# A delta-rule layer's triangular inverse: its 16x16 diagonal blocks solved on VectorE through memory, TensorE's doublings from 16 on

## The reference, cut to what matters

```python
a_mat = jnp.where(strict, jnp.einsum("bhncd,bhnmd->bhncm", kb, k) * decay, 0.0)
t_mat = a_mat + jnp.eye(cs, dtype=f32)
rhs = jnp.concatenate([v * beta[..., None], kb * jnp.exp(gc)[..., None]], axis=-1)
sol = lax.linalg.triangular_solve(t_mat, rhs, left_side=True, lower=True, unit_diagonal=True)
...
v_new = u_i - jnp.einsum("bhcd,bhde->bhce", w_i, s)
o_i = jnp.einsum("bhcd,bhde->bhce", q_i, s) + jnp.einsum("bhcm,bhme->bhce", qk_i, v_new)
s = s * d_i[..., None, None] + jnp.einsum("bhcd,bhce->bhde", k_i, v_new)
```

## Time and profile before

| what | value |
| --- | --- |
| median of 3 runs | 3300.11 us (3296.35 to 3301.86) |
| profiled execution: its own time | 3295.26 us |
| its span, first to last instruction | 3293.5 us |
| mean granted TensorE clock | 0.976 |
| TensorE (PE) matmul busy | 3108.8 us, 94% of the span |
| TensorE weight load (PEld) busy | 2038.3 us, 62% |
| VectorE (DVE) busy | 1745.3 us, 53% |
| ScalarE (ACT) busy | 1522.9 us, 46% |
| GpSimd (POOL) busy | 775.7 us, 24% |
| DMA engines, mean share | 24.6% |
| masked copies of the inverse on VectorE (L1319, L1321) | 502.8 us |

### The profile page before, as it was taken

How to read it: one execution, slowest core, us unless ns; L and a number is a source line. 1 busy time by engine, 2 the same in 40 slices (tenths; PEclk the granted TensorE clock), 3 DMA queues, 4 the chain that set the end, 5 groups by cost and what they waited for, 6 DMA issues and landing times. The chain is left out here.

```text
span 3293.5 us, 56323 instructions
## 1 busy us (share of the span) xinstructions
PE 3108.8 (94%) x22057; PEld 2038.3 (62%) x22057; DVE 1745.3 (53%) x3545; ACT 1522.9 (46%) x3283; POOL 775.7 (24%) x588
## 2 busy tenths in 40 slices
PE   5878999999999999999999999796999999999998
PEld 2346777777777764455545565443777777777753
DVE  1136666666666652244442344344667767766632
ACT  3135555555555541145532444333556555555521
POOL 0033433333343220001101011003343434343300
PEclk9689999999999999999999999998999999999999
DMA  9911211221121027012302111202122212121135
GB/s 375 321 56 44 70 51 56 60 60 56 48 73 56 29 70 264 3 53 63 132 18 49 33 46 41 82 11 72 49 62 64 64 52 72 52 75 53 43 118 191
DMA packets 224099, 261.97 MB, mean 80 GB/s; under 512 B 19418, under 2 KB 158948, under 8 KB 223716
## 3 DMA queue, kind: packets, MB, share of 16 engines
q1 hardware_dynamic: 223844, 258.46, 24.6%
HBM read 239.15 MB, written 19.27 MB: 78 GB/s over the span
## 5 line engine op out<-in xcount | busy, mean ns | idle before, releaser
L894 PE MATMUL ps<-hT,W 128*128 128x512 f32 (+1 forms) x2656 | 997.4, 506 | 3.2 <-DVEq L192 2.0
L894 PEld LDWEIGHTS ps<-hT,W 128*128 128x128 f32 x2656 | 470.4, 192 | 200.8 <-issue 171.6
L1319 DVE CAST_PREDICATED arena<-mask,ps 128x384 bf16<-128x384 uint32 x448 | 252.6, 564 | 201.7 <-PE ps L963 166.2
L1144 ACT CAST arena<-ps 128x384 bf16<-128x384 f32 x384 | 167.0, 482 | 339.0 <-PE ps L950 338.0
L2355 PE MATMUL ps<-arena 128*128 128x512 f32 x712 | 309.5, 592 | 2.6 <-SPq L192 2.4
L1321 DVE CAST_PREDICATED arena<-mask,ps 128x384 bf16<-128x384 uint32 x448 | 250.2, 558 | 0.0
L2355 PEld LDWEIGHTS ps<-arena 128*128 128x128 f32 x712 | 133.9, 190 | 166.4 <-issue 161.7
L1990 PE MATMUL ps<-hT,W 128*128 128x512 f32 (+1 forms) x608 | 218.2, 493 | 0.8 <-DMA W<-in_att_w_in 0.5
L1431 POOL TENSOR_TENSOR arena<-arena,cst 128x768 f32<-128x768 f32 x64 | 117.1, 1852 | 386.6 <-DVE arena L1288 384.0
L1300 DVE SCALAR_TENSOR_TENSOR arena<-arena,vec 128x770 f32<-128x770 f32 (+1 forms) x192 | 196.2, 1022 | 6.8
L961 PEld LDWEIGHTS ps<-arena 128*128 128x128 bf16 x2304 | 153.1, 98 | 42.4 <-issue 32.5
(11 more groups left out here) (279 smaller groups left out, 6112.5 us busy)
## 6 DMA issues: line engine op xcount, KB each, us to landing
arena<-in_ada_w SPq DMA_DIRECT2D x24, 2048.0 KB, 19.5
W<-in_gdn_w_in SPq DMA_DIRECT2D x95, 512.0 KB, 4.0
arena<-decay_sums SPq DMA_DIRECT2D x64, 384.0 KB, 4.1
W<-decay_rows SPq DMA_DIRECT2D x64, 384.0 KB, 5.1
arena<-in_gdn_w_out SPq DMA_DIRECT2D x32, 512.0 KB, 10.6
W<-in_gdn_w_out SPq DMA_DIRECT2D x30, 512.0 KB, 3.5
arena<-gated SPq DMA_DIRECT2D x32, 384.0 KB, 8.0
gated<-arena SPq DMA_DIRECT2D x24, 384.0 KB, 2.3
```

The source lines that it names most:

```text
L894: mm = pe.matmul(ps[:, b, 0:t1 - t0], w[:, i, :], env.hT[:, i, t0:t1], start=(i == 0), stop=(i == KD - 1))
L1144: act.copy(half_cols(Xb[d], s, d), ps[:, 2 * d, 0:384].rearrange("p (c b s) -> p c b s", c=NT, s=s)).then_inc(*inxe.up(m, lv, d))
L1319: dve.copy_predicated(half_cols(Mb[d], s, d), wide(env.m4[:, d, lv]), src_m).then_inc(*inm.up(m, lv, d, "m"))
```

## The change

Levels 0 to 3 leave TensorE. In their place the inverses of all 16x16 diagonal blocks of a unit (48 for each direction, 96 in all) are computed on VectorE, a block in each partition. To get there, SP stores `NAT[0]` and the blockwise transpose of `NAT[1]` (`flip`, one VectorE transpose in 32x32 tiles, into `flipped`, which lies where a piece of the refinement lies later) to memory, and loads the 16x16 blocks back, a block in a partition (`blocks_out`). `solve` does 14 steps of a multiplication and an addition each, every one dependent on the one before, at program steps 3, 4 and 5, behind the scan's part of the step. Two casts make bf16 blocks and their transposes; SP stores them into matrices in memory whose off-diagonal parts were cleared once, and loads `Mb` and `MTb` whole from there (`blocks_in`). TensorE goes on with levels 4 to 6 at steps 9 to 14 as before, after a wait for these loads. GpSimd no longer copies identities, and splits `NAT` only after the solving and the stores. `FILL` puts more fill into steps 2 to 8 and less into 9 to 16. The memory arrays have a row pitch of 129 rows a chunk, so that the diagonal blocks are equally spaced. The masks for levels 0 to 3 and the signals that belong to them are gone (not shown), and the two pieces `XLb` and `NLLb` lie in the arena in another way.

```diff
+FIRST_LEVEL = 4
+BLK = 1 << FIRST_LEVEL
+NBLK = NT * (P // BLK)
+PITCH = P + 1
...
+SOLVE_AT = {3: (1, 6), 4: (6, 11), 5: (11, BLK - 1)}
-FILL = (5, 5, 4, 5, 5, 4, 5, 5, 3, 5, 5, 4, 5, 5, 5, 4, 7, 0)
+FILL = (5, 5, 5, 6, 6, 5, 6, 6, 5, 4, 4, 4, 4, 4, 4, 4, 6, 0)
...
+                    ("blk", (BLK, BLK)), ("prod", (BLK, BLK)), ("diagb", (2, BLK, BLK))])
+    XLb, NLLb = ([flat(t).bitcast(BF16)[:, i * T:(i + 1) * T].rearrange("p (c n) -> p c n", c=NT) for i in range(2)] for t in v.MF)
+    flipped = v.MF[0]
...
+        def blocks(dram):
+            return dram.rearrange("c p n -> (c p n)").rearrange("(k x) -> k x", k=NBLK)[:, 0:BLK * P].rearrange("k (r n) -> k r n", n=P)[:, :, 0:BLK]
+        def rows(dram):
+            return dram[:, 0:P, :].rearrange("c p n -> p c n")
+        def blocks_out(m):
+            sp.wait_ge(natd.sem, natd.at(m, 0))
+            sp.dma_start(rows(a["nat"][0]), NAT[0]).then_inc(*nat_out.up(m, 0))
+            sp.wait_ge(turned.sem, turned.at(m))
+            sp.dma_start(rows(a["nat"][1]), flipped).then_inc(*nat_out.up(m, 1))
+            sp.wait_ge(nat_out.sem, nat_out.at(m, 1))
+            for d in BOTH:
+                sp.dma_start(v.blk[NBLK * d:NBLK * (d + 1)], blocks(a["nat"][d])).then_inc(*blk_in.up(m, d))
+        def blocks_in(m):
+            sp.wait_ge(diag_in.sem, diag_in.at(m - 1, 1, 1))
+            sp.wait_ge(solved.sem, solved.at(m, "cols"))
+            for k in range(2):
+                for d in BOTH:
+                    sp.dma_start(blocks(a["inv"][k, d]), v.diagb[NBLK * d:NBLK * (d + 1), k ^ 1 ^ d]).then_inc(*diag_out.up(m, k, d))
+            sp.wait_ge(diag_out.sem, diag_out.at(m, 1, 1))
+            sp.wait_ge(rf.sem, rf.at(m - 1, "t3", 1))
+            for k, t in enumerate((Mb, MTb)):
+                for d in BOTH:
+                    sp.dma_start(t[d], rows(a["inv"][k, d])).then_inc(*diag_in.up(m, k, d))
         if l:
             ahead(sp)
+        else:
+            sp.wait_ge(t_set.sem, t_set.at("xb0"))
+            for k in range(2):
+                for d in BOTH:
+                    sp.dma_start(rows(a["inv"][k, d]), Xb[0]).then_inc(*cleared.up(k, d))
+            sp.wait_ge(cleared.sem, cleared.at(1, 1))
...
                 for d in BOTH:
                     sp.dma_start(flat(QD[m % 2][d]), a["rows"][d, m].partition_broadcast(P)).then_inc(*eg.up(m, d))
+            if m in U:
+                blocks_out(m)
             if n + 3 in U:
                 sp.wait_ge(gcap.sem, gcap.at(n + 2, 1))
...
                 sp.wait_ge(ad.sem, ad.at(n, "X1"))
                 load_x(n + 1)
+            if m in U:
+                blocks_in(m)
             if n == GU - 1:
...
-            if p == 2:
-                for d in BOTH:
-                    pe.wait_ge(natb.sem, natb.at(m, d))
-                    pe.wait_ge(mtf.sem, mtf.at(m - 1, d))
-                    icol = env.identb[:].rearrange("p (b two s) -> p b two s", two=2, s=1)[:, :, d, :]
-                    for c in range(NT):
-                        pe.matmul(ps[:, 2 * d, c * 64:(c + 1) * 64].rearrange("p (b s) -> p b s", s=1),
-                                  NATb[d][:, c], icol, start=True, stop=True)
-                    mm = pe.matmul(ps[:, 2 * d + 1, 0:384], env.identb[:],
-                                   NATb[d].rearrange("p c (b two) -> p (c b) two", two=2)[:, :, 1 - d], start=True, stop=True)
-                    mm.then_inc(*inx.up(m, 0, d))
-            elif p < 15 and p % 2:
+            if p < 2 * FIRST_LEVEL + 1:
+                return
+            if p < 15 and p % 2:
                 lv = (p - 1) // 2
                 s = 1 << lv
                 for d in BOTH:
-                    pe.wait_ge(inm.sem, inm.at(m, lv - 1, d, "t"))
+                    if lv == FIRST_LEVEL:
+                        pe.wait_ge(natb.sem, natb.at(m, d))
+                        pe.wait_ge(mtf.sem, mtf.at(m - 1, d))
+                        pe.wait_ge(diag_in.sem, diag_in.at(m, 1, 1))
+                    else:
+                        pe.wait_ge(inm.sem, inm.at(m, lv - 1, d, "t"))
                     mcol = half_cols(Mb[d], s, d)
...
-                elif p < 15 and p % 2:
+                elif 2 * FIRST_LEVEL < p < 15 and p % 2:
...
-            if p < 15:
+            if p < 2 * FIRST_LEVEL + 2:
+                return
+            elif p < 15:
                 lv = (p - 2) // 2
                 s = 1 << lv
...
+        def flip(m):
+            dve.wait_ge(natd.sem, natd.at(m, 1))
+            dve.wait_ge(rf.sem, rf.at(m - 1, "t1", 1))
+            dve.transpose(flat(flipped), flat(NAT[1])).then_inc(*turned.up(m))
+        blk, prod = v.blk[0:2 * NBLK], v.prod[0:2 * NBLK]
+        def solve(m, lo, hi):
+            if lo == 1:
+                dve.wait_ge(blk_in.sem, blk_in.at(m, 1))
+                dve.memset(flat(blk)[:, ::BLK + 1], 1.0).then_inc(*solved.up(m, "one"))
+            for t in range(lo, hi):
+                left = blk[:, 0:t, t:t + 1].broadcast_to([2 * NBLK, t, BLK - 1 - t])
+                row = blk[:, t:t + 1, t + 1:BLK].broadcast_to([2 * NBLK, t, BLK - 1 - t])
+                out, part = blk[:, 0:t, t + 1:BLK], prod[:, 0:t, t + 1:BLK]
+                if t > 1:
+                    dve.wait_ge(solved.sem, solved.at(m, (t - 1, "add")))
+                dve.tensor_tensor(part, left, row, ALU.mult).then_inc(*solved.up(m, (t, "mul")))
+                dve.wait_ge(solved.sem, solved.at(m, (t, "mul")))
+                dve.tensor_tensor(out, out, part, ALU.add).then_inc(*solved.up(m, (t, "add")))
+            if hi == BLK - 1:
+                dve.wait_ge(solved.sem, solved.at(m, (BLK - 2, "add")))
+                dve.wait_ge(diag_out.sem, diag_out.at(m - 1, 1, 1))
+                dve.tensor_copy(v.diagb[0:2 * NBLK, 0], blk).then_inc(*solved.up(m, "rows"))
+                dve.tensor_copy(v.diagb[0:2 * NBLK, 1], blk.rearrange("p a b -> p b a")).then_inc(*solved.up(m, "cols"))
...
             for p in range(POS):
+                if p == 0 and m in U:
+                    flip(m)
                 if p == 0 and n in U:
                     score(n)
...
+                if p in SOLVE_AT and m in U:
+                    solve(m, *SOLVE_AT[p])
...
-        def ones_on_diagonal(m):
-            for d in BOTH:
-                pool.wait_ge(rf.sem, rf.at(m - 1, "r0", d))
-                pool.tensor_copy(Mb[d], idb).then_inc(*minit.up(m, d, "m"))
-            for d in BOTH:
-                pool.wait_ge(m1.sem, m1.at(m - 1, d))
-                pool.tensor_copy(MTb[d], idb).then_inc(*minit.up(m, d, "t"))
         capped(0)
-        ones_on_diagonal(0)
         for n in SLOTS:
             m = n + 1
             if m in U:
+                pool.wait_ge(solved.sem, solved.at(m, "cols"))
                 for d in BOTH:
                     pool.wait_ge(natb.sem, natb.at(m, d))
+                    pool.wait_ge(nat_out.sem, nat_out.at(m, 1))
                     pool.tensor_tensor(NAT[d], NAT[d], NATb[d], ALU.subtract).then_inc(*nlo.up(m, d, "rest"))
...
-            if m in U and m + 1 in U:
-                ones_on_diagonal(m + 1)
...
+    aps["nat"] = nc.dram_tensor("nat_rows", (2, NT, PITCH, P), F32).ap()
+    aps["inv"] = nc.dram_tensor("diag_blocks", (2, 2, NT, PITCH, P), BF16).ap()
```

More of the change, by code:

```diff
@@ L74, in shape_constants @@
     cst = np.concatenate([ident, ones, upper, lower, cap_f, cap_b, perm, cos, sin, band], axis=1)
-    mask = np.zeros((P, 2, LEVELS, P // 2), np.uint32)
-    for lv in range(LEVELS):
+    mask = np.zeros((P, 2, LEVELS - FIRST_LEVEL, P // 2), np.uint32)
+    for lv in range(FIRST_LEVEL, LEVELS):
         blk = r >> lv
@@ L81, in shape_constants @@
             cols = blk[blk % 2 == par]
-            mask[:, par, lv, :] = blk[:, None] == (cols + (1 if par == 0 else -1))[None, :]
+            mask[:, par, lv - FIRST_LEVEL, :] = blk[:, None] == (cols + (1 if par == 0 else -1))[None, :]
     return cst.astype(np.float32), mask.reshape(P, -1)
 CST_W = 7 * P + 2 * SEQ + 3 * P
-MASK_W = 2 * LEVELS * P // 2
+MASK_W = 2 * (LEVELS - FIRST_LEVEL) * P // 2
 class Sig:
@@ L164, in build @@
         env.band = env.cst[:, 7 * P + 2 * SEQ:]
-        env.m4 = env.mask[:].rearrange("p (two l c) -> p two l c", two=2, l=LEVELS)
+        env.m4 = env.mask[:].rearrange("p (two l c) -> p two l c", two=2, l=LEVELS - FIRST_LEVEL)
         env.held = ctx.enter_context(nc.semaphore("held"))
@@ L637, in gdn_phase @@
                     ("Xb", (NT, P), 2), ("NATb", (NT, P), 2), ("Mb", (NT, P), 2), ("MTb", (NT, P), 2), ("NLOb", (NT, P), 2), ("nidb", (P,)),
-                    ("gexp", (2, T), 3), ("table", (4 * NT * 2, 16))])
-    XLb, NLLb = ([flat(t).bitcast(BF16)[:, i * T:(i + 1) * T].rearrange("p (c n) -> p c n", c=NT) for t in v.MF] for i in range(2))
+                    ("gexp", (2, T), 3), ("table", (4 * NT * 2, 16)),
+                    ("blk", (BLK, BLK)), ("prod", (BLK, BLK)), ("diagb", (2, BLK, BLK))])
```

(24 more changed lines are left out.)

9 lines of the change are left out of this document (removed).

## The result

The change makes the kernel slower by 0.9%: 3325.39 us, median of 5 runs (3322.3 to 3335.75), against 3300.11. The ratio, taken from the means of the runs, is 1.0093, with a 95% interval of 1.0069 to 1.0117 (the medians alone would give 1.0077). It is a small loss, but clear of the noise. The range held it, the sign was wrong. The profiled execution has a span of 3323.6 us against 3293.5, +30.1, where the sum had -25.

A forecast was written before the change was run, and what follows sets the result against it. TensorE's own work was taken to bound the delta-rule slots. Layer 0 -46, layer 3 +13 and +2, first slots +6 gave -25 us on 3295.26: 3270, or 3275 as median; range 3205 to 3365.

The forecast's parts named there:

- the sum: Whole kernel: layer 0 -46, layer 3 +13 and +2, first slots +6; total -25 us, so faster.
- The chain's end: Solved blocks back from memory for TensorE's step 9: +28.9 us from slot start in layer 0, +28.2 in layer 3.
- The other end of the arithmetic: Layer 0 slot: arrival 28.9 plus 31.3 us left behind it, 60.2 against 63.3.
- Other edits: GpSimd's split after the solving ends by 33.7 us, squares by 36; without cover until step 12 it costs its lateness.
- is no fuller: VectorE loses 9.0 us of predicated copies a slot and gains 8.7 us of other work.
- Cover: TensorE's work before step 9: 28.1 us in layer 0, 22.5 and 24.0 in layer 3; what follows shrinks by 2.6.
- V: Theory formed after measuring: VectorE is late since the moved split stands beside its convolution; no chance given.
- Rival C: Layer 3's waits drop TensorE's clock to half for 3 to 5 us, +22 to +38: 3297 to 3313; chance 0.15.
- C: Theory formed after measuring: the memory chain is late at step 9, above all in layer 3, and the clock falls behind.
- B: Tiny block packets cost 20 ns like 256 B ones, +86 us, 3361; decides from 13 ns a packet; chance 0.17.
- D: Stored packets under 512 B cost as much as whole ones, 38 ns, +144 us, 3420; chance 0.06.
- A: Chain through memory shorter by 3 us, stores behind the tail and tiny packets free: -88, 3212; chance 0.14.

The follow-up runs named there:

- e14: Changed kernel with the FILL of the kernel before, six cost units of fills back behind step 9; 3403.13 us, ratio 1.0328.
- e5: Changed kernel with GpSimd's split touching only 8 columns for all but each layer's first unit; 3312.72 us, ratio 1.0048.
- e15: Changed kernel with e5's 8-column split and three thrown-away TensorE products ahead of layer 3's wait at step 9; 3290.24 us, ratio 0.9983.
- e12: Changed kernel, both layers: GpSimd's split between squares and decay sums, odd slots' matrix at step 16, M loaded before its transpose; 3363.54 us, ratio 1.0202.
- e3: Changed kernel with M loaded and waited for ahead of its transpose, which is awaited at step 10; 3310.34 us, ratio 1.0028.
- e7: e3 with VectorE's gating moved from step 9 to step 10, behind level 4's copies; 3286.37 us, ratio 0.9968.
- e8: The change in layer 0 alone, layer 3 as in the kernel before; 3276.13 us, ratio 0.9948.
- e10: e8 with e7's edits in layer 0: M loaded first, gating behind level 4's copies; 3254.36 us, ratio 0.9876.

## Why the prediction was wrong

**What held, and what was luck.** The chain's end held: arrival at +28.6 and +28.1 for a forecast of 28.9 and 28.2, the solving's operations 0.195 and 0.197 us on average, the transpose 0.975 (1.0 was taken). Its terms held less well, and part of that is luck. In the odd slot of layer 0 with its zero at 824.66 the loads of the blocks left at +7.1 (9.0 was said), the solving began at +10.2 (11.4) and ended at +19.7 (20.4), the stores took 3.7 (3.2) and the loads of M 5.2 (5.3): the way out was priced 1.9 too high, the blocks' loads 0.7, the solving 0.5 and the stores 0.5 too low. TensorE was ready for step 9 at +28.5 there (28.1), so that the 3.9 us a unit less and the 2.6 of the moved fills held together; e14 shows the fills alone. The other end of the arithmetic held too: e5's layer 0 at 60.18 for 60.2.

**The step that failed** is in "Other edits": GpSimd's later split was costed only at its own end ("From 20.4 that ends by 33.7 ... and step 12 asks for them"), as if nothing stood beside it. The same paragraph had the evidence: L1349 took 3.27 us for two beside GpSimd, and I booked the relief there as a gain (it came: 1.78 for two L1424) without asking what VectorE does at the split's new place. It does the convolution. That VectorE "is no fuller" failed with it: VectorE's busy time rose from 1745.3 to 1861.2 us, and with the split small (e5) it is 1695.6. Measured: 1.5 us a slot in layer 0 (e5 against after), 21.7 us over 14 slots, which is nearly all of layer 0's miss.

**The second step that failed** is the last of "Cover": what is left behind step 9 "shrinks by the same 2.6", 28.5 and 29.0 in layer 3. It measured 33.7 and 30.3 there, by V, the falls of the clock and a wait at the refinement, and this is more than all of layer 3's 2.5 us a slot.

**Rival C happened**, with a chance of 0.15, but the time isn't its 3297 to 3313, and it wasn't the whole: nine falls in 770 us, 3.4 us each at half clock, 15.4 us lost. What I had against it ("part of the wait is paid earlier") was true: TensorE waits 14.2 us in all at step 6 for L1440. It didn't save the clock. How layer 3's miss of 2.5 us a slot splits between V and C has no single answer, since they hide each other: each removed alone gave 0.3 and 0.0, both 1.5 (e15). The last 1.0 of it is still there in e15. It is a wait of 2.0 us at the refinement (L1023 for L1368) in the odd slots, 15.5 us in the changed kernel, 14.5 in e15 and 3.8 in e14; in the kernel before it was
```profile
PE ps L973 <- DVE arena L1321: 3.1, 8, 1.0
```
Since e14 changes nothing but the fills, the fills moved ahead were cover for VectorE there.

**Rivals B and D** fell. The 3136 packets of the blocks' stores kept 16 engines busy for 40.5% of 3.8 us, 196 on each, 7.9 ns a packet of 32 B (10 was taken, B needs 13). The reading, changing and writing of small stores that the Trainium skill states (DMA: Bandwidth & Descriptors, Specifications) shows no price here. **A** fell with the arrival: no chain came 3 us earlier.

**The sign.** With V and the falls out (e15) the profiled execution has -47.5 in layer 0, +22.7 in layer 3 and +17.3 elsewhere, where the sum had -46, +15 and +6: the terms hold but for some 20 us. Of those, 11 lie outside the 28 slots. The two first slots are 4.2 and 6.9 us longer, where the sum had 3 each; the rest there wasn't looked into. Layer 3 won in no run that solves its blocks: with the whole split in it the best is 57.78 a slot (e12), against 56.35 before. In the changed kernel TensorE is ready for its step 9 after 23 to 26 us and the chain needs 26 to 29. With M loaded first (e3, e7, e12) that wait is all but gone and layer 3 still loses 1.4 to 2.2 us a slot, now in waits for VectorE and in the clock; what it would be with VectorE in time there no run shows. Layer 0 alone wins (e8, e10). What layer 3 pays was in my sum (+15), only too small.

## What to carry to other kernels

When work of GpSimd is moved, lay it beside VectorE's program at the new place. In these traces VectorE's operations on SBUF waited there for the end of a whole GpSimd instruction (0.2 us became 1.7), and those that read PSUM didn't; the worst neighbour was the chain of small operations. If the two must meet, put first what TensorE waits for (e10). When a loop body's chain replaces work on the bound engine, compare chain and cover for each layer by itself, and cost what lies behind the chain's end as well: work moved ahead of it was cover for something there. Keep the change only where it wins. Two causes that hide each other each test as nothing: before a cause is dropped because its removal gave nothing, remove it together with the other.
